# One 512-column matmul in place of two of 256 for the high part of the weights, its second half spilled and summed, in the gate, up and down projections of a two-block network on one core

## The reference

```python
def swiglu_ffn(h, w_gate_up, w_down):
    gu = h @ w_gate_up
    g, u = jnp.split(gu, 2, axis=-1)
    return (jax.nn.silu(g) * u) @ w_down          # D_FF = 2816

bcx = h @ w_in                                     # 1024 x 3072: b_gate, c_gate, xv
u = b_gate * xv; y = conv(u); mix = (c_gate * y) @ w_out
```

```python
u = rms_norm(h, mlp_pre_norm[l])
m = jnp.square(jax.nn.relu(u @ w_mlp_up[l])) @ w_mlp_down[l]      # 1024 x 4096, 4096 x 1024
h = h + rms_norm(m, mlp_post_norm[l])
```

## Time and profile before

| | before |
|---|---|
| median of 3 runs | 1063.49 us |
| the profiled execution | 1065.07 us, of it 1063.3 us from the first to the last instruction |
| TensorE matmul busy | 1024.0 us (96%), 8424 matmuls |
| TensorE weight loads busy | 1012.5 us (95%), 8424 |
| VectorE busy | 692.6 us (65%), 994 instructions |
| ScalarE busy | 565.4 us (53%), 933 |
| GpSimd busy | 286.8 us (27%), 256 |
| DMA | 181.01 MB, mean 170 GB/s |

### The profile page before, as it was taken

The page is one execution under the profiler, slowest core; times in us unless marked ns, Lnnn a source line. Parts: engine busy times, 40 slices in busy tenths (PEclk is TensorE's granted clock), DMA queues, the critical chain, the costliest instruction groups (busy, mean ns, idle before and its releaser), DMA issues.

```text
span 1063.3 us, 22713 instructions
## 1 busy us (share of the span) xinstructions
PE 1024.0 (96%) x8424; PEld 1012.5 (95%) x8424; DVE 692.6 (65%) x994; ACT 565.4 (53%) x933; POOL 286.8 (27%) x256
## 2 busy tenths in 40 slices
PE   8999999999997799999999999799999999999995
PEld 8999999999996599999999999799999989999995
DVE  6787666666567747666655799467766767554443
ACT  5455544445454756444444566766474556554331
POOL 2231232220000422332201069601031434441111
PEclk9999999999999899999999999899999999999998
DMA  8675455445553025545445454444444525555421
GB/s 307 228 288 188 173 190 191 169 173 189 189 195 122 2 80 198 185 170 197 165 170 208 181 180 156 156 172 134 148 162 165 201 106 198 178 178 198 174 105 40
DMA packets 26564, 181.01 MB, mean 170 GB/s; under 512 B 3072, under 2 KB 4224, under 8 KB 6144
## 3 DMA queue, kind: packets, MB, share of 16 engines
q1 hardware_dynamic: 26496, 180.07, 47.0%
HBM read 179.01 MB, written 1.05 MB: 169 GB/s over the span
## 4 chain that ended last, share of the span: by engine, by line
PE 89%; POOL 4%; DVE 3%; ACT 3%; issue 1%; DMA 1%; SPq 0%; POOLq 0%; DVEq 0%; ACTq 0%
PE bank L374 29%; PE bank L375 28%; PE bank L376 28%; POOL rtmp L1592 2%; POOL rtmp L1594 1%; ACT pr L886 1%; DMA raw<-in_stream 1%; DVE mx L1322 1%; DVE z L1466 1%; POOL k L1598 0%; POOL q L1598 0%; DVE wlo L1092 0%; ACT whi L711 0%; DVE mx L1315 0%; PE bank L614 0%
## 5 line engine op out<-in xcount | busy, mean ns | idle before, releaser
L1092 DVE TENSOR_TENSOR wlo<-raw,whi 128x1024 fp32r<-128x1024 f32 (+1 forms) x336 | 414.4, 1234 | 245.0 <-ACT whi L711 243.8
L711 ACT ACTIVATE whi<-raw 128x1024 fp32r<-128x1024 f32 (+2 forms) x336 | 351.8, 1048 | 388.2 <-PE bank L376 382.0
L374 PE MATMUL bank<-xa,whi 128*128 128x256 f32 x1760 | 504.2, 286 | 3.8 <-DVE xa L1120 2.0
L375 PE MATMUL bank<-xa,whi 128*128 128x256 f32 x1760 | 498.6, 283 | 0.0
L376 PE MATMUL bank<-xa,wlo 128*128 128x256 f32 x1760 | 498.5, 283 | 0.0
L374 PEld LDWEIGHTS bank<-xa,whi 128*128 128x128 f32 x1760 | 338.1, 192 | 5.5 <-issue 2.4
L375 PEld LDWEIGHTS bank<-xa,whi 128*128 128x128 f32 x1760 | 338.3, 192 | 0.3
L376 PEld LDWEIGHTS bank<-xa,wlo 128*128 128x128 f32 x1760 | 338.3, 192 | 0.0
L375 PE MATMUL bank<-hid,whi 128*128 128x256 f32 x608 | 171.1, 281 | 0.0
L374 PE MATMUL bank<-hid,whi 128*128 128x256 f32 x608 | 171.1, 281 | 0.0
L376 PE MATMUL bank<-hid,wlo 128*128 128x256 f32 x608 | 171.1, 281 | 0.0
(11 more groups left out here) (198 smaller groups left out, 888.8 us busy)
## 6 DMA issues: line engine op xcount, KB each, us to landing
raw<-in_stream SPq DMA_DIRECT2D x158, 1024.0 KB, 4.8
raw<-in_stream SPq DMA_DIRECT2D x8, 768.0 KB, 4.3
bias<-in_bias SPq DMA_DIRECT2D x1, 3072.0 KB, 12.0
raw<-in_stream SPq DMA_DIRECT2D x4, 512.0 KB, 7.9
x<-in_x SPq DMA_DIRECT2D x2, 512.0 KB, 6.1
out<-x SPq DMA_DIRECT2D x8, 128.0 KB, 1.9
cons<-in_cons SPq DMA_DIRECT2D x1, 640.0 KB, 9.1
vecs<-in_vecs SPq DMA_DIRECT2D x1, 77.0 KB, 1.9
```

The lines of the kernel that those rows point to most:

```text
L374: pe.matmul(dst, whi[:, slot, at + i, :], X[:, k, 0, :], start=first and i == 0, stop=False)
L375: pe.matmul(dst, whi[:, slot, at + i, :], X[:, k, 1, :], start=False, stop=False)
L711: act.activation(whi[:, p, 0:kts, :].rearrange("p k m -> p (k m)"), src, ACT.Copy)\
L1092: dve.tensor_tensor(wlo[:, p, 0:kts, :].rearrange("p k m -> p (k m)"), src, whi[:, p, 0:kts, :].rearrange("p k m -> p (k m)").bitcast(F32) ...
```

## The change

Where a stage is in `S0` (`bx`, `up0`, `dn0`, `up1`, `dn1`, `mup`, `mdn`), the two matmuls with high weights become one of 512 columns: `X[:, k, :, :]` goes through the array against one load of `whi`, into all 512 columns of the bank. Blocks are taken in pairs: high, high, rest, rest. In the other stages (`c`, `o`, `qkv`, `x2` and so on) `blocks` makes the same matmuls in the new order. When a wide bank is done, ScalarE copies its columns 256:512 into `spill`, and VectorE adds `spill` to the columns 0:256 into `z` (or `mres`), which empties the bank; the product that emptied it before is then made on `z` in SBUF. In a down projection the leading chunks are wide in banks 0 and 1, and the last chunk (8, 6 or, in `mdn`, 8 blocks) stays with three matmuls of 256 columns, in banks 2 and 3; the sum of the leading chunks is added to `x` by GpSimd (`dn0`, `dn1`) or kept in `mres`, and the last chunk is added to it.

```diff
-TILES = {"bx": 16, "c": 8, "o": 8, "up0": 44, "dn0": 8, "qkv": 12, "wo": 8, "up1": 44, "dn1": 8,
+TILES = {"bx": 16, "c": 8, "o": 8, "up0": 44, "dn0": 16, "qkv": 12, "wo": 8, "up1": 44, "dn1": 16,
...
+S0 = {}
+for _name in ("bx", "up0", "dn0", "up1", "dn1", "mup", "mdn"):
+    S0[_name] = _s
+    _s += KT if _name in ("dn0", "dn1", "mdn") else TILES[_name]
...
+        spill = sb("spill", [P, 4, TOK])
...
             def blocks(slot, X, tiles, dst, first, last, at=0):
-                for i, k in enumerate(tiles):
-                    pe.matmul(dst, whi[:, slot, at + i, :], X[:, k, 0, :], start=first and i == 0, stop=False)
-                    pe.matmul(dst, whi[:, slot, at + i, :], X[:, k, 1, :], start=False, stop=False)
-                    ins = pe.matmul(dst, wlo[:, slot, at + i, :], X[:, k, 0, :],
-                                    start=False, stop=last and i == len(tiles) - 1)
+                narrow = dst[:, 0:TOK]
+                for i0 in range(0, len(tiles), 2):
+                    pair = [(i, tiles[i]) for i in range(i0, min(i0 + 2, len(tiles)))]
+                    for i, k in pair:
+                        if dst.shape[1] == 2 * TOK:
+                            pe.matmul(dst, whi[:, slot, at + i, :], X[:, k, :, :], start=first and i == 0, stop=False)
+                        else:
+                            pe.matmul(narrow, whi[:, slot, at + i, :], X[:, k, 0, :], start=first and i == 0,
+                                      stop=False)
+                            pe.matmul(narrow, whi[:, slot, at + i, :], X[:, k, 1, :], start=False, stop=False)
+                    for i, k in pair:
+                        ins = pe.matmul(narrow, wlo[:, slot, at + i, :], X[:, k, 0, :],
+                                        start=False, stop=last and i == len(tiles) - 1)
...
-                    if c == 0:
+                    if c != 1:
                         pe.wait_ge(emptied, tile - 3)
-                    blocks(n % 4, hid, range(k0, k0 + kts), acc(tile), c == 0, c == 2)\
+                    blocks(n % 4, hid, range(k0, k0 + kts), acc(tile, c < 2), c != 1, c >= 1)\
...
+            def spill_tile(n, slot):
+                act.wait_ge(piece_done, n + 1)
+                act.activation(spill[:, slot, :], bank[slot][:, TOK:2 * TOK], ACT.Copy).then_inc(spilled, 1)
...
+                        spill_tile(4 * (B0[name] + i) + p, p)
                         round_weights(B0[name] + i + 1, p)
...
+            def sum_tile(at, slot, dst):
+                dve.wait_ge(spilled, at + 1)
+                dve.tensor_tensor(dst, acc(slot), spill[:, slot, :], ALU.add).then_inc(emptied, 1)
+            def scale_sum(tile, at, slot):
+                dve.wait_ge(emptied, tile + 1)
+                dve.tensor_tensor(z[:, slot, :], z[:, slot, :], rbc[:], ALU.mult).then_inc(scaled, 1)
...
+                        sum_tile(S0[name] + 4 * i + p, p, z[:, p, :])
                         if p < 2:
-                            scale_tile(n, p, z[:, p, :])
+                            scale_sum(tile, SCALED[name], p)
                         else:
-                            dve.wait_ge(piece_done, n + 1)
+                            dve.wait_ge(emptied, tile + 1)
                             dve.wait_ge(gate_ready, base + 2 * i + p - 1)
-                            dve.tensor_tensor(z[:, p, :], acc(p), gate[:, p - 2, :], ALU.mult).then_inc(emptied, 1)
+                            dve.tensor_tensor(z[:, p, :], z[:, p, :], gate[:, p - 2, :], ALU.mult)\
+                               .then_inc(hval_ready, 1)
...
+                    if c == 1:
+                        sum_tile(S0[name] + t, m, z[:, m, :])
                     if c == 2:
-                        add_residual(4 * B0[name] + q, t, T0[name] + t)
+                        dve.wait_ge(pre_added, (0 if name == "dn0" else 8) + t + 1)
+                        add_residual(4 * B0[name] + q, t, 2 + m)
...
+                    sum_tile(S0["mup"] + 4 * i + p, p, z[:, p, :])
+                    dve.wait_ge(emptied, T0["mup"] + 4 * i + p + 1)
+                    dve.scalar_tensor_tensor(out=z[:, p, :], in0=z[:, p, :], scalar=0.0, in1=rbc[:],
+                                             op0=ALU.max, op1=ALU.mult).then_inc(relu_ready, 1)
...
+                if q // 2 % 4 == 2:
+                    sum_tile(S0["mdn"] + t, q % 2, mres[:, t, :])
                 if q // 2 % 4 == 3:
                     dve.wait_ge(piece_done, 4 * B0["mdn"] + q + 1)
-                    dve.tensor_copy(mres[:, t, :], acc(T0["mdn"] + t)).then_inc(emptied, 1)
+                    dve.wait_ge(emptied, T0["mdn"] + 4 * (q // 8) + q % 2 + 1)
+                    dve.tensor_tensor(mres[:, t, :], acc(2 + q % 2), mres[:, t, :], ALU.add).then_inc(emptied, 1)
...
+            def down(name, norm):
+                for t in range(KT):
+                    if t % 2 == 0:
+                        for s in (t, t + 1):
+                            pool.wait_ge(emptied, T0[name] + 2 * t + s - t + 1)
+                            pool.tensor_tensor(x[:, s, :], x[:, s, :], z[:, s - t, :], ALU.add).then_inc(pre_added, 1)
+                    add_square(t, norm)
```

More of the change, by code:

```diff
@@ L279, in build @@
                  "mpre": 92, "hid2": 100}
+        SCALED = {"bx": 0, "up0": 16, "up1": 38}
         NORM = {"mix0": 0, "ffn0": 1, "mix1": 2, "ffn1": 3, "pre2": 4, "post2": 5, "mpre": 6, "mpost": 7}
@@ L457, in body @@
                         pe.wait_ge(emptied, T0[name] + 4 * (1 + i) + p - 3)
-                        blocks(p, X, range(8), acc(p), True, True).then_inc(piece_done, 1)
+                        blocks(p, X, range(8), acc(p, name in S0), True, True).then_inc(piece_done, 1)
                 repeat(pe, count, body)
@@ L692, in _ @@
                     pe.wait_ge(split_lo, SPLIT["hid2"] + (24 if q == 0 else 32))
-                if c == 0:
+                if c in (0, 3):
                     pe.wait_ge(emptied, tile - 3)
-                blocks(n % 4, hid, range(8 * c, 8 * c + 8), acc(tile), c == 0, c == 3)\
+                blocks(n % 4, hid, range(8 * c, 8 * c + 8), acc(tile, c < 3), c in (0, 3), c >= 2)\
                     .then_inc(piece_done, 1)
@@ L1048, in up_hi @@
             def up_hi(tile, slot):
-                act.wait_ge(emptied, T0["mup"] + tile + 1)
+                act.wait_ge(relu_ready, tile + 1)
                 if not isinstance(tile, int) or tile >= 4:
@@ L1059, in squared_up @@
                         rms(NORM["mpre"])
+                    spill_tile(4 * (B0["mup"] + i) + p, p)
                     round_weights(B0["mup"] + i + 1, p)
@@ L1516, in _, with add_square @@
         def _(pool):
-            def add_squares(norm):
-                for t in range(1, 7 if norm in TURNED else 8):
+            def add_square(t, norm):
+                if 1 <= t < (7 if norm in TURNED else 8):
                     pool.wait_ge(squared, 8 * norm + t + 1)
@@ L1526, in add_squares @@
                         pool.tensor_tensor(ssum[:], ssum[:], sq[:, t % 2, :], ALU.add).then_inc(sq_added, 1)
+            def add_squares(norm):
+                for t in range(KT):
+                    add_square(t, norm)
+            def down(name, norm):
+                for t in range(KT):
+                    if t % 2 == 0:
+                        for s in (t, t + 1):
+                            pool.wait_ge(emptied, T0[name] + 2 * t + s - t + 1)
+                            pool.tensor_tensor(x[:, s, :], x[:, s, :], z[:, s - t, :], ALU.add).then_inc(pre_added, 1)
+                    add_square(t, norm)
             def gates(name, norm, layer):
@@ L1561, in _ @@
             gates("up0", NORM["ffn0"], 0)
-            add_squares(NORM["mix1"])
+            down("dn0", NORM["mix1"])
             def attention_lo(i):
@@ L1582, in _ @@
             gates("up1", NORM["ffn1"], 1)
-            add_squares(NORM["pre2"])
+            down("dn1", NORM["pre2"])
             def rope(j):
```

46 lines of the change are left out of this document (28 added, 18 removed).

## The result

The changed kernel takes 1049.07 us in the median of 4 runs (1047.56 to 1052.54), beside 1063.84 for the kernel before on the same chip: a ratio of 0.9865, interval 0.984 to 0.9891. It is 14.8 us faster (by the interval 11.6 to 17.0), where 35.1 were forecast: the sign is right, the size less than half, and 1049 lies above the range of 1010 to 1047. The profiled execution took 1052.54 us with a span of 1050.7.

The account below looks back on a forecast made before the run. TensorE's stream of matmuls, busy for 96% of the span, was taken as the bound. Wide matmuls -35.6 us and the start of `mup` +0.5 gave -35.1, from 1063.5 to 1028.4 us; range 1010 to 1047.

Parts of the forecast that it names:

- I take 0.216: In the wide blocks: a 512-column fp32r matmul takes 0.216 us, so 1536 blocks give 35.6 us less.
- the order in pairs I cost at nothing: In the blocks: pairing costs nothing, as the loads are as many and each still lies behind one matmul.
- The fixed price: Rival on every fp32r matmul: 0.0133 us each, wide or not; wide one 0.2267, gain 19.8 us, time 1044.2; chance 20%.
- the 0.0133 us above the columns: In narrow matmuls at full clock: 0.120 us taken where columns need 0.1067; 0.0133 is something other than columns.
- the row that was nearest in length: Line 405: six matmuls 0.216 us apart, each with its own 128x128 load, taken to price the wide matmul.
- The rate of the moving operand: Rival on fp32r columns out of SBUF: 256 per 0.120 us, wide matmul 0.240, nothing gained, time 1064.0; chance 12%.
- VectorE as the bound: Rival in the 22 gate and up bodies: VectorE takes 13.2 us per body, time 1082; chance 5%.
- the third rival: On the narrow rest matmuls: they may fall to 0.108 us, block 0.324, 53.5 us less, time 1010.5; chance 6%.
- no new waits of TensorE inside the loops: In the loops: spill, sum, additions and DMA queue add nothing to TensorE's waits; such waits for VectorE would refute the prediction.
- the `mup` restart: At the start of `mup`: the spill goes ahead of the rounding and delays TensorE's restart, +0.5 us.
- the fixed price with some stalls: Whole kernel: the case that sets the slow end of the range, 1047.
- the upper bound that I named for `xa`, 0.240: In the wide blocks on `xa`: one wide matmul takes at most as long as two narrow ones, 0.240 us.

Follow-up runs that it names:

- the doubled sum: The changed kernel with each of the 160 VectorE sums of bank and spill made twice; ratio to the kernel before 0.9867 (0.9851 to 0.9884).
- the probe: A program of matmuls alone, network left out: plain fp32 of 256 and 128 columns, and blocks in the earlier order; rows 0.2158 and 0.1117, blocks 0.3600 us.
- the first probe: A program of matmuls alone, network left out, by width and type, quiet and beside busy engines; fp32r of 512 columns 226.7 ns, of 256 columns 120.0.

## Why the prediction was wrong, and what in it was right

**What failed is the step "I take 0.216" for the wide matmul, and with it, four times smaller, "the order in pairs I cost at nothing".** In a stream of its own the wide matmul takes 0.2267, in pairs 0.233 with the narrow one beside it at 0.115. The forecast gain, 35.1 us, was 20.3 too high. The fixed price makes 1536 x 0.0107 = 16.4 of it. The other 4 come from the change of width, which makes a block in pairs 0.3483 and not 0.2267 + 0.120, a block in the first bodies 0.353, and from `hid`, where a pair costs 0.349 and not 0.2267 + 0.1186.

The sum with the measured pitches: 960 blocks on `xa` by 0.360 - 0.3483 = 0.0117 are 11.2 us; 128 blocks in the first bodies, which are made one at a time and take 0.353, are 0.9; 448 on `hid` by 0.3559 - 0.349 = 0.0069 are 3.1. Together 15.2, less 0.3 at `mup`: 14.9 us. The medians show 14.8, and their interval is too wide for so close an agreement to be more than luck; the stages bear it out better. From first to last matmul `up0` and `up1` take 123.10 for 127.01, `dn0` and `dn1` 61.66 for 62.54, `mup` 93.24 for 95.59 and `mdn` 89.62 for 91.02: 13.3 us less. `bx`, with the half-clock stretch in it, shows nothing in this profile, and 1.3 less in that of the doubled sum, which has no such stretch.

**The row was there and was read the wrong way.** I held the 0.0133 us above the columns for a trace of the weight load that a long matmul would hide, and took the price from the row that was nearest in length. That row is plain fp32. The rows of line 411 are plain fp32 as well, take about as long as the columns of a narrow fp32r matmul, and have a load of the same length: they are 0.108 apart. If the load made all of the 0.0133, it would have shown there. So the row said that a good part of the price goes with the type, and I used it against the fixed price. It said so less sharply than the 0.108 looks: the probe has 0.1117 for the same shape, 5.0 ns above the columns, and narrower weights take half of the narrow matmul's 13 ns. For the wide one the probes leave no doubt: with loads of equal length plain fp32 pays 2.5 ns and fp32r 13.4. "Nearest" has to be judged by what the disputed quantity may hang on, not by duration.

**The Trainium skill**, page "TensorE: Matmul & The Clock Gate", section "Back-to-back issue gap", gives N / 2.4 + 2.5 ns for a warm matmul and names no type. The runs agree for bf16 (109.2 and 215.8) and disagree for fp32r (120.0 and 226.7).

**The rivals.** The fixed price, given 20%, is what happened: its mechanism, its 0.2267 (measured 0.2267) and its time, 1044.2, are nearest. It is 5 us too fast, because it too costed the order at nothing (its 0.0133 for a block on `xa` came out as 0.0117 and, in the first bodies, 0.007) and expected 0.0119 on `hid`, where a pair saves 0.0069. The rate of the moving operand is refuted by the first probe, and VectorE as the bound by the doubled sum. The narrow ones do gain, as the third rival had it, but 0.115 in pairs and not 0.108, and the wide ones next to them lose a little more than that.

**What held:** 1536 matmuls fewer; spill and sum at 0.382 and 0.422 (0.384 and 0.415 taken) and hidden; 8.9 us of VectorE per body; the product on `z` at 0.43; no new waits of TensorE inside the loops; the `mup` restart as the one place without slack, 0.32 in place of 0.5.

**The range** ended at 1047 with "the fixed price with some stalls". A case of 20% whose own bounds were worked out no further than its middle left the range too short on that side: the same rival with the wide one at the upper bound that I named for `xa`, 0.240, joins it to the rate case at 1064, and the chances called for that.

## What to carry to other kernels

From 256 to 512 columns the pitch of a matmul had a part per column and a part per instruction; at 128 columns that sum did not hold. The second part goes with the data type: to price a shape that the trace does not have, take the part per instruction from rows of the same type, and test whether the load is its cause on a row with the same array time and the same load. An edit that joins two matmuls in one saves that part once, less what changing width costs; where wide and narrow ones must alternate, try pairs. And look where a new step falls behind another for no need at a place without slack: here the spill could go before the norm, and the sum before the rest of the weights, at no cost.

## What the runs showed of the hardware

- An fp32r matmul of 256, 384 or 512 columns takes 13.3 to 13.4 ns above its columns at full clock; bf16 of 256 and 512 columns takes 2.5. At half clock fp32r takes its columns alone (0.64 us for 768).
- A plain fp32 matmul leaves two rows, each with a load; a row of 256 columns takes 215.8 ns and one of 128 columns 111.7. An fp32r matmul of 128 columns takes 111.7 too.
- The row of a 128x128 load is 188 to 192 ns long in fp32r and plain fp32, and 98 in bf16.
- After a change from narrow to wide the wide matmuls take 233, 236, 228, 233, 231 ns and only then 227; from wide to narrow the first takes 114.
- Fewer weight columns make a narrow fp32r matmul faster (113.4 for 120.0, with 64 as with 32) and a wide one slower (229.8 and 231.7 for 226.7). What in the engine makes the fixed price is not settled.
- With all engines busy and 422 GB/s of DMA the pitches of matmuls do not move (120.0 for 256 columns, 348 for a block in pairs).
